# One decoder layer on one Trainium2 core: page-table reads spread among weight loads, state-space units with decays built in TensorE's weights, norms from a block of ones

## The chip, the core and the metric

The kernel runs on one core of one Trainium2 chip. A core has TensorE (PE, matrix products into PSUM), VectorE (DVE), ScalarE (ACT), GpSimd (POOL) and SyncE (SP), which here issues nearly all DMAs. Each engine runs its own instruction stream in order, and semaphores tie the streams together. The metric is the device time of one execution in microseconds (us), lower is better.

## The reference

One decoder layer for 512 prompt tokens and 8 samples of 8 new tokens (576 tokens, width 2048), all in fp32: one projection, sparse attention on one half of the heads, a Mamba-2 scan (SSD) on the other, an output projection, and a convolutional feed-forward layer, with RMS norms around both halves. Cut to what the change touches:

```python
def rmsnorm(x, g):
    y = x * lax.rsqrt(jnp.mean(x * x, -1, keepdims=True) + EPS)
    return y * g

def nsa_sample(...):                      # paged cache, 8 samples x 4 pages
    past = cache_kv_l[page_table].reshape(b, past_len, N_CACHE_SLOTS, KV_HEADS, HEAD_DIM)
    ...
    return o, win_all[:, -win_len:]       # win_sample: cache rows moved on by 8, and the new ones

# nsa_block, compressed branch: scores of every query with 31 blocks
s_c = jnp.einsum('btgrd,bngd->btgrn', q, kc) * SCALE + bias_c

def ssd_scan(x, a, bm, cm, h0):           # step, chunk of 128 tokens
    acum = jnp.cumsum(ac, axis=1)
    seg = acum[:, :, None] - acum[:, None]
    decay = jnp.where(causal, jnp.exp(jnp.where(causal, seg, 0.0)), 0.0)
    cb = jnp.einsum('bign,bjgn->bijg', cc, bc)
    y = jnp.einsum('bijg,bijgr,bjgrp->bigrp', cb, decay, xc)
    y = y + jnp.einsum('bign,bgrpn->bigrp', cc, h) * jnp.exp(acum)[..., None]
    h = (h * jnp.exp(acum[:, -1])[..., None, None]
         + jnp.einsum('bjgn,bjgrp->bgrpn', bc, xc * to_end[..., None]))

# block_tail
x = x + rmsnorm(mix, g_mix_post)
h = rmsnorm(x, g_ffn_pre)
```

## The kernel before

`build()` writes the whole layer as five streams by hand. Tokens are in five tiles (four of 128 rows, one of 64), or in two halves of 288 columns where features lie on partitions. Counters called `phase` join the engines between stages. The order within a stage is that of the code.

**Weight stream.** A weight unit is 128 rows of 512 columns. SP loads unit u into one of four buffers, once the low part of unit u-4 has been made (`unit`, L425 on). ACT makes the high part (L697), after PE has finished unit u-1; POOL makes the low part, and PE does three matmuls for one product (high x high, low x high, high x low). The stages with most time are these: `w_in`, then `w_out` (L2041), then the feed-forward layer (L1609 to L1611, L2119). The period is PE's.

**Page table.** After the last weight load of `w_in`, SP reads the 32 entries of the page table into registers (L456), one `value_load` each, then waits for phase 8 and loads the old states of the scan in 8 parts (L466). The registers are used later, for the loads of the cache rows.

**State loop.** For each of the 8 parts PE transposes the states (L1714), ACT copies them (L775), PE multiplies them with C for the samples (L1724), and multiplies `B_by_sequence` with `x_to_end` for the new states (L1740, 64 rows, 512 columns); DVE adds, SP stores. `B_by_sequence` is made by POOL (L1517), last in a chain of products that begins once the exps of ACT (L770) are there. DVE's copies before these exps (L1090, L1091) take the cumulated decays out of PSUM; the first goes into `a_cumulative`.

**SSM units.** 20 units w = 4 tile + group, each for four heads. `ssd_scores(w)`: PE makes C B^T (L1752, 128x128) and, per head, the cumulated decay over all partitions (L1754: weights are the column a of the head, broadcast, times a triangle of ones). `seg_unit(w)`: DVE subtracts `a_cumulative` and adds a mask of 0 and -1e30 (L1116, four operations). ACT takes the exp in place (L797). `mix_unit(w)`: DVE multiplies `seg` (SBUF) with the scores in PSUM (L1124). `ssd_out(w)`: PE makes the output (L1766), the part from the state (L1769) and the new state (L1771), in banks 4, 5 and 6, after `unit_done(w-1)`. `out_unit(w)`: DVE scales and adds (L1142 to L1147: five operations, two for tile 0 and for the samples). POOL gates the result with z (L1526), and ACT's `unit_squares(w)` (L791) sums the squares. DVE's order is seg(w), out(w-1), mix(w). PE's is scores(w+1), out(w). POOL makes three products of 128x1024 for the next tile (L1499, L1501, L1507) at each tile boundary. Two buffers of `seg` and of the banks alternate.

**Compressed scores.** For the prompt PE multiplies queries and 31 compressed keys: 16 heads x 4 tiles, 64 rows each, in two records per product (L1956). A pair of KV heads lies in the upper and lower 64 partitions (row group q = 0 or 64). The order is by head, so four products in a row use one row group. Four heads share a bank and one signal `C_mm`, after which DVE adds the bias and subtracts the maximum (L1303 to L1306). Ahead of that DVE fills `bias_c` (L1294, L1298) out of `bias_p`, which DMAs bring.

**Middle norms.** In the last block of `w_out` ACT squares each finished block of 128 features (L662) and DVE sums 15 of 16 (L1376). `square_sums` (L2051) then makes ten matmuls with a column of ones, which give the sums with tokens on partitions; `rs_small` (L1361 to L1365) divides by D, adds eps and inverts; ACT takes the root of 128x5 values (L925); `rs_rows2` (L2059) spreads them back over all partitions and into rows by five matmuls with the unit matrix. DVE's L1385 and L1386 use them. The second norm does the same with one sum (L1391, L2051, L1363 on, L961, L2059), and L1404 copies the rows to SBUF. An fp32 matmul shows as two records.

**Copies.** The 8 parts of `win_sample` that are taken over from the cache are DMAs of 1008 KB each from memory to memory, on SP's queue before the `w_out` loads (L541 to L543).

## Time and profile before

| | us |
| --- | --- |
| median of 3 runs | 3338.15 |
| the runs | 3348.89, 3338.15, 3336.52 |
| the profiled execution | 3346.54 |
| its span in the trace | 3344.4 |
| PE busy in it | 3109.9 (93%) |
| DVE, ACT, POOL busy | 1110.9, 1096.3, 1117.3 (33% each) |
| TensorE clock, mean | 0.942 of full |

The span runs from the first to the last instruction in the trace; 2.14 us lie outside. PE is busy nearly all the time in the weight stages. The middle stages lie from about 625 (end of the `w_in` stream) to 1366 (start of the `w_out` stream), and the middle norms at 1581 to 1655. A row of a timeline tells the start, the length, the engine, the line, the operation, output and inputs, how many were merged into the row, and in square brackets how long the engine idled before it and what released it. Times in this section's rows are us from the start of the span.

### The profile page before, as it was taken

How to read it: one execution, taken by the hardware profiler on the slowest of the kernel's cores; microseconds unless marked ns; L12 is line 12 of the kernel's file. 1: busy time of each engine (PE TensorE's matmuls, PEld its weight loads, DVE VectorE, ACT ScalarE, POOL GpSimd, SP SyncE). 2: the span in 40 equal slices, each digit the busy share in tenths (PEclk: the TensorE clock that was granted, in tenths of full speed). 3: DMA queues.
4: the chain of work that ended last, by engine and by line, in shares of the span. 5: the costliest groups of instructions: out<-in, count | busy, mean ns of one | idle time of the engine just before them, and what ended most of it. 6: DMA issues, size and time to landing. Idle time of an engine off the chain costs nothing.

```text
span 3344.4 us, 56486 instructions
## 1 busy us (share of the span) xinstructions
PE 3109.9 (93%) x21753; PEld 2893.2 (87%) x21753; DVE 1110.9 (33%) x1924; ACT 1096.3 (33%) x1980; POOL 1117.3 (33%) x911
## 2 busy tenths in 40 slices
PE   8999998977788789899799999999999999999997
PEld 7999776756685556799799999999999999999997
DVE  3145000016433365211532333323232333434344
ACT  4222222311223266322633333333333333333332
POOL 2444333223001022233444444444444434343342
PEclk9999999957698799999899999999999999999998
DMA  6333223131343700322322222222222222222233
GB/s 184 83 82 82 76 75 106 38 92 41 74 110 121 197 1 2 107 79 81 95 82 82 82 82 82 83 83 82 82 82 82 82 75 83 78 82 78 76 120 112
DMA packets 385732, 285.23 MB, mean 85 GB/s; under 512 B 95549, under 2 KB 321949, under 8 KB 384270
## 3 DMA queue, kind: packets, MB, share of 16 engines
q1 hardware_dynamic: 382152, 275.50, 29.1%
q10 hardware_dynamic: 3472, 8.26, 0.7%
q8 instruction: 71, 1.16, 0.2%
q14 instruction: 37, 0.30, 0.0%
HBM read 259.98 MB, written 31.97 MB: 87 GB/s over the span
## 4 chain that ended last, share of the span: by engine, by line
PE 67%; issue 16%; POOL 6%; DVE 4%; SPq 4%; ACT 3%; DMA 0%; POOLq 0%; DVEq 0%; ACTq 0%
PE ps L2119 17%; PE ps L1609 11%; PE ps L1611 11%; PE ps L1610 11%; POOL w_lo L1488 5%; PE ps L2041 5%; SPq L456 1%; SPq L521 1%; PE ps L2003 1%; PE ps L1969 1%; PE ps L1922 1%; ACT scores_p L883 1%; PE ps L1740 1%; ACT pT_prompt L894 1%; PE ps L1724 1%
## 5 line engine op out<-in xcount | busy, mean ns | idle before, releaser
L1560 POOL TENSOR_TENSOR w_lo<-w_raw,w_hi 128x512 fp32r<-128x512 f32 x572 | 737.3, 1289 | 1158.5 <-ACT w_hi L975 656.5
L1609 PE MATMUL ps<-hT_hi,w_hi 128*128 128x288 f32 x3520 | 1048.0, 298 | 3.4 <-DVE ffn_xr L1415 2.8
L1610 PE MATMUL ps<-hT_lo,w_hi 128*128 128x288 f32 x3520 | 1041.0, 296 | 0.0
L1611 PE MATMUL ps<-hT_hi,w_lo 128*128 128x288 f32 x3520 | 1037.3, 295 | 0.0
L1609 PEld LDWEIGHTS ps<-hT_hi,w_hi 128*128 128x128 f32 x3520 | 662.1, 188 | 5.2 <-POOL w_lo L1560 3.0
L1611 PEld LDWEIGHTS ps<-hT_hi,w_lo 128*128 128x128 f32 x3520 | 665.5, 189 | 0.0
L1610 PEld LDWEIGHTS ps<-hT_lo,w_hi 128*128 128x128 f32 x3520 | 663.5, 188 | 0.0
L975 ACT ACTIVATE w_hi<-w_raw 128x512 fp32r<-128x512 f32 x336 | 213.2, 635 | 716.8 <-PE ps L1611 716.8
L1488 POOL TENSOR_TENSOR w_lo<-w_raw,w_hi 128x512 fp32r<-128x512 f32 x176 | 233.1, 1325 | 397.8 <-ACT w_hi L697 397.8
L697 ACT ACTIVATE w_hi<-w_raw 128x512 fp32r<-128x512 f32 x250 | 157.9, 633 | 616.5 <-PE ps L1611 216.7
L680 DVE TENSOR_TENSOR act_lo<-ffn_act_T,act_hi 128x576 fp32r<-128x576 f32 x172 | 219.6, 1277 | 332.6 <-ACT act_hi L673 332.6
L2119 PE MATMUL ps<-act_hi,w_hi 128*128 128x288 f32 x1376 | 298.0, 299 | 15.4 <-DVE ffn_out_T L1440 10.7
L2119 PE MATMUL ps<-act_lo,w_hi 128*128 128x288 f32 x1376 | 297.7, 298 | 0.0
L2119 PE MATMUL ps<-act_hi,w_lo 128*128 128x288 f32 x1376 | 297.2, 298 | 0.0
L2119 PEld LDWEIGHTS ps<-act_hi,w_hi 128*128 128x128 f32 x1376 | 224.6, 191 | 16.2 <-issue 16.2
L671 ACT ACTIVATE w_hi<-w_raw 128x512 fp32r<-128x512 f32 x172 | 108.8, 632 | 360.2 <-PE ps L2119 353.2
L2119 PEld LDWEIGHTS ps<-act_lo,w_hi 128*128 128x128 f32 x1376 | 224.6, 191 | 0.0
L2119 PEld LDWEIGHTS ps<-act_hi,w_lo 128*128 128x128 f32 x1376 | 224.4, 191 | 0.0
L1669 PE MATMUL ps<-w_hi,hT_hi 128*128 128x512 f32 (+1 forms) x400 | 158.7, 397 | 16.0 <-POOL w_lo L1488 9.2
L1670 PE MATMUL ps<-w_hi,hT_lo 128*128 128x512 f32 (+1 forms) x400 | 157.4, 394 | 0.0
L1671 PE MATMUL ps<-w_lo,hT_hi 128*128 128x512 f32 (+1 forms) x400 | 156.1, 390 | 0.0
L1428 DVE TENSOR_TENSOR ffn_act_T<-ps,rs_rows_sb 128x576 f32 x43 | 32.6, 757 | 297.3 <-PE ps L1611 297.3
(368 smaller groups left out, 3888.4 us busy)
## 6 DMA issues: line engine op xcount, KB each, us to landing
w_raw<-in_ffn_w_gate SPq DMA_DIRECT2D x172, 256.0 KB, 2.8
w_raw<-in_ffn_w_up SPq DMA_DIRECT2D x172, 256.0 KB, 2.8
w_raw<-in_ffn_w_down SPq DMA_DIRECT2D x172, 256.0 KB, 2.6
w_raw<-in_w_in SPq DMA_DIRECT2D x144, 256.0 KB, 2.7
w_raw<-in_w_out SPq DMA_DIRECT2D x64, 256.0 KB, 2.6
w_raw<-in_w_in SPq DMA_DIRECT2D x64, 128.0 KB, 2.7
cmp_rows<-in_cache_kv SPq DMA_DIRECT2D x64, 128.0 KB, 3.2
kv_rows<-in_cache_kv SPq DMA_DIRECT2D x32, 256.0 KB
```

Of the source, the lines that this page charges most:

```text
L680: dve.tensor_tensor(a_lo[:, v % 2, :], src, a_hi[:, v % 2, :].bitcast(F32), ALU.subtract).then_inc(alo_done, 1)
L697: act.activation(w_hi[:, u % 2, :], w_raw[:, u % 4, :], ACT.Copy).then_inc(hi_done, 1)
L975: act.activation(w_hi[:, j % 2, :], w_raw[:, (U_FFN + j) % 4, :], ACT.Copy).then_inc(hi_done, 1)
L1488: pool.tensor_tensor(w_lo[:, j % 2, :], w_raw[:, j, :], w_hi[:, j % 2, :].bitcast(F32), ALU.subtract).then_inc(lo_done, 1)
L1560: pool.tensor_tensor(w_lo[:, u % 2, :], w_raw[:, u % 4, :], w_hi[:, u % 2, :].bitcast(F32), ALU.subtract).then_inc(lo_done, 1)
L1609: pe.matmul(o, W[0], X[0], start=(k == 0), stop=False)
L1610: pe.matmul(o, W[0], X[1], start=False, stop=False)
L1611: i = pe.matmul(o, W[1], X[0], start=False, stop=(k == KT - 1))
L1669: pe.matmul(o, X[0], W[0], start=(k == 0), stop=False)
L1670: pe.matmul(o, X[1], W[0], start=False, stop=False)
L2041: m = pe.matmul(ps[:, 2 * f + h, 0:HALF], W[wt], mix[:, k, HALF * h:HALF * h + HALF], start=(k == 0 and x == 0), stop=False, skip_group_ch ...
L2119: m = pe.matmul(ps[:, 2 * f + h, 0:HALF], W[wt], act_[:, v % 2, HALF * h:HALF * h + HALF], start=(k == 0 and x == 0), stop=False, skip_gro ...
```

## The change

1. The 32 reads of the page table stand behind one weight load each, for the units of c = 1 and 2 of the `w_in` stream, and no longer behind the last load.
2. In the SSM units the seg(w) of DVE is gone. ACT writes, per head, `decay_weights`: a mask of ones for k > i, times the head's a (`Copy` with a scale per partition, four operations of 128x128). PE uses it as weights against the triangle, so that PSUM holds the sum of a over the tokens between. ACT takes the exp from PSUM into `seg`. DVE's new `mask_unit` multiplies the scores with the triangle into `masked_scores`, and mix(w) multiplies two SBUF operands. DVE's order is mask(w), mix(w), out(w-1); ACT's is decay_weights(w+1), exp(w), squares(w-1). `ssd_out` alternates between banks 4 and 5, 6 and 7, and waits for `unit_done(w-2)`. The two copies to `a_cumulative` are gone.
3. The middle norms multiply the squares with a 128x128 block of ones, in two halves of 288 columns, which gives the sum on all partitions at once (ten matmuls for the first norm, over the sum of 12 squares and the last four; two for the second). ACT takes the root over 128x576 in PSUM with scale 1/D and bias eps; DVE takes the reciprocal over 128x576. The small matmuls, the small DVE operations and L1376 for the last three blocks go.
4. The eight copies of `win_sample` stand behind every eighth `w_out` load.
5. The compressed scores alternate between the row groups with each product. Banks 0 and 1 are signalled half way, banks 2 and 3 at the end.
6. The load of the sample gates counts on the same semaphore as the bias loads.

```diff
@@ SP
+            pages = [[None] * 4 for s in range(NB)]
             for c in range(5):
                 col = O_KV + 512 * c if c < 3 else O_Z + 512 * (c - 3)
                 for k in range(KT):
                     unit(U_KV + KT * c + k, dram(w_in, k * 128 * INW + col, [[INW, 128], [1, 512]]), 0)
+                    if 1 <= c < 3:
+                        s, p = 4 * (c - 1) + k // 4, k % 4
+                        pages[s][p] = sp.value_load(A["page_table"][s:s + 1, p:p + 1], min_val=0, max_val=39)
...
-            pages = [[sp.value_load(A["page_table"][s:s + 1, p:p + 1], min_val=0, max_val=39) for p in range(4)] for s in range(NB)]
...
                     unit(U_OUT + KT * c + k, dram(A["w_out"], k * 128 * D + 512 * c, [[D, 128], [1, 512]]), 0)
+                    if k % 8 == 4:
+                        s = 2 * c + k // 8
+                        sp.dma_start(O["win_sample"][0, s, 0:PAST - NT].rearrange("t s g d -> t (s g d)"),
+                                     A["cache_win_kv"][0, s, NT:PAST].rearrange("t s g d -> t (s g d)")).then_inc(y_stored, 16)
@@ ACT
+            def decay_weights(w):
+
+                t, g = w // 4, w % 4
+                n = TILES[t][1]
+                later = con[0:n, C_SL:C_SL + n] if t < 4 else con[0:n, C_SLS:C_SLS + n]
+                if w >= 2:
+                    act.wait_ge(s1_ready, w - 1)
+                for h in range(4):
+                    i = act.activation(decw[0:n, w % 2, h, 0:n], later, ACT.Copy, scale=a_[0:n, t, 4 * g + h:4 * g + h + 1])
+                i.then_inc(decw_ready, 1)
+
+            act.wait_ge(a_ready, 1)
+            decay_weights(0)
             for w in range(20):
                 n = TILES[w // 4][1]
-                act.wait_ge(seg_ready, w + 1)
-                act.activation(seg[0:n, w % 2, :, 0:n], seg[0:n, w % 2, :, 0:n], ACT.Exp).then_inc(dec_exp, 1)
+                if w < 19:
+                    decay_weights(w + 1)
+                act.wait_ge(s1_ready, w + 1)
+                if w >= 2:
+                    act.wait_ge(y_ready, w - 1)
+                act.activation(seg[0:n, w % 2, :, 0:n], ps[0:n, 2 + w % 2, :].rearrange("p (h i) -> p h i", h=4)[:, :, 0:n], ACT.Exp).then_inc(dec_exp, 1)
                 if w:
                     unit_squares(w - 1)
...
-            act.wait_ge(inv_ready, 2)
-            act.activation(rs, rs, ACT.Sqrt).then_inc(rs_ready, 1)
+            act.wait_ge(sum3_ready, 1)
+            act.activation(ps[:, 0:2, 0:HALF], ps[:, 0:2, 0:HALF], ACT.Sqrt, scale=1.0 / D, bias=eps_col).then_inc(rs_ready, 1)
@@ DVE
+            def mask_unit(w):
...
+                dve.tensor_tensor(scm[0:n, w % 2, 0:n], ps[0:n, w % 2, 0:n], earlier, ALU.mult).then_inc(scm_ready, 1)
...
                 dve.tensor_tensor(seg[0:n, w % 2, :, 0:n], seg[0:n, w % 2, :, 0:n],
-                                  ps[0:n, w % 2, 0:n].unsqueeze(1).broadcast_to([n, 4, n]), ALU.mult).then_inc(M_done, 1)
+                                  scm[0:n, w % 2, 0:n].unsqueeze(1).broadcast_to([n, 4, n]), ALU.mult).then_inc(M_done, 1)
...
             for w in range(21):
                 if w < 20:
-                    seg_unit(w)
+                    mask_unit(w)
+                    mix_unit(w)
                 if w >= 1:
                     out_unit(w - 1)
-                if w < 20:
-                    mix_unit(w)
...
-            dve.wait_ge(sum3_ready, 1)
-            rs_small(0)
-            dve.wait_ge(few_T, 6)
+            dve.wait_ge(rs_ready, 2)
             dve.wait_ge(y_evac, 16)
+            ch(dve.reciprocal(halves(flat(6)), ps[:, 0:2, 0:HALF]))
@@ PE
+                pe.wait_ge(decw_ready, w + 1)
...
-                    i = pe.matmul(ps[0:n, 2 + w % 2, 128 * h:128 * h + n], a_[0:n, t, 4 * g + h:4 * g + h + 1].broadcast_to([n, n]), tri, start=True, stop=True)
+                    i = pe.matmul(ps[0:n, 2 + w % 2, 128 * h:128 * h + n], decw[0:n, w % 2, h, 0:n], tri, start=True, stop=True)
...
+            for x in range(8):
                 for i in range(4):
...
+                    for par in range(2):
+                        h = 8 * (x // 4) + 4 * par + x % 4
+                        g, q = h // 4, 64 * par
...
+            def square_sums(bank, sq, first, last):
+
+                for h in range(2):
+                    i = pe.matmul(ps[:, bank + h, 0:HALF], every, sq[:, HALF * h:HALF * h + HALF], start=first, stop=last, skip_group_check=True)
+                if last:
+                    i.then_inc(sum3_ready, 1)
```

ACT's order in the SSM units before: `seg` is the exp of a unit, `squares_unused` the squares of the one before.

```order
L782 ACTIVATE ssd_small<-ps 128x8
L797 ACTIVATE seg<-seg 128x512 x2
L791 ACTIVATE squares_unused_88,ssd_small<-zs 128x256
L797 ACTIVATE seg<-seg 128x512
L791 ACTIVATE squares_unused_88,ssd_small<-zs 128x256
```

The same place now, where `decay_weights` are the four activations of a unit:

```order
L788 ACTIVATE ssd_small<-ps 128x8
L808 ACTIVATE decay_weights<-con,ssd_small 128x128 x8
L820 ACTIVATE seg<-ps 128x512
L808 ACTIVATE decay_weights<-con,ssd_small 128x128 x4
L820 ACTIVATE seg<-ps 128x512
L797 ACTIVATE squares_unused_89,ssd_small<-zs 128x256
L808 ACTIVATE decay_weights<-con,ssd_small 128x128 x4
L820 ACTIVATE seg<-ps 128x512
```

Between the squares of one unit and the exp of the next stand four activations that weren't there.

DVE in a unit of the tiles 1 to 3 before, from the subtraction of unit w over the five output operations of unit w-1 to its mix:

```order
L1116 SCALAR_TENSOR_TENSOR seg<-ps,a_cumulative,con 128x128 x4
L1142 TENSOR_TENSOR y_tmp<-ps,ssd_small 128x256
L1143 TENSOR_TENSOR h_state<-h_state,ssd_small 128x256
L1144 TENSOR_TENSOR xs_tok<-xs_tok,ps 128x256
L1146 TENSOR_TENSOR h_state<-h_state,ps 128x256
L1147 TENSOR_TENSOR xs_tok<-xs_tok,y_tmp 128x256
L1124 TENSOR_TENSOR seg<-seg,ps 128x512
```

And now:

```order
L1139 TENSOR_TENSOR masked_scores<-ps,con 128x128
L1146 TENSOR_TENSOR seg<-seg,masked_scores 128x512
L1164 TENSOR_TENSOR y_tmp<-ps,ssd_small 128x256
L1165 TENSOR_TENSOR h_state<-h_state,ssd_small 128x256
L1166 TENSOR_TENSOR xs_tok<-xs_tok,ps 128x256
L1168 TENSOR_TENSOR h_state<-h_state,ps 128x256
L1169 TENSOR_TENSOR xs_tok<-xs_tok,y_tmp 128x256
```

The mix has moved ahead of the output operations of the unit before, behind one product in place of four subtractions.

SP where the KV weights are loaded, now; before, all of these `TENSOR_LOAD` rows stood behind the last weight load:

```order
L435 DMA w_raw<-in_w_in 128x512 x17
L454 TENSOR_LOAD in_page_table_ptr
L454 TENSOR_LOAD in_page_table
L454 ISA x2
L435 DMA w_raw<-in_w_in 128x512
L454 TENSOR_LOAD in_page_table_ptr
```

One read stands between two loads of 128x512.

## Rows read from the trace of the kernel before

**Rows 1.** The page's chain of waits, by line: share of the span.

```profile
PE ps L2119 17%; PE ps L1609 11%; PE ps L1611 11%; PE ps L1610 11%; POOL w_lo L1488 5%; PE ps L2041 5%; SPq L456 1%; SPq L521 1%; PE ps L2003 1%; PE ps L1969 1%; PE ps L1922 1%; ACT scores_p L883 1%; PE ps L1740 1%; ACT pT_prompt L894 1%; PE ps L1724 1%
```

**Rows 2.** Timeline of SP, 620 to 690.

```profile
624.90 0.58 SPq L453 DMA_DIRECT2D w_raw<-in_w_in  x1
681.60 0.36 SPq L460 DMA_DIRECT2D norm_gain<-in_ssm_norm_g  x1
```

**Rows 3.** Timeline of PE, 664 to 701.

```profile
667.74 0.26 PE L1707 MATMUL ps<-ssd_small,con 64*64 64x16 f32 x2
688.12 1.94 PE L1714 MATMUL ps<-con,h 128*128 128x128 f32 x8 [20.12 <-DMA h<-in_state_ssm]
...
697.11 3.78 PE L1740 MATMUL ps<-B_by_sequence,x_to_end 64*128 64x512 f32 x4
```

**Rows 4.** Timeline of ACT in the w_in stream.

```profile
377.61 0.63 ACT L697 ACTIVATE w_hi<-w_raw 128x512 fp32r<-128x512 f32 x1 [2.80 <-PE ps L1671]
```

**Rows 5.** Timeline of POOL, 674 to 700.

```profile
679.53 1.89 POOL L1517 TENSOR_TENSOR B_by_sequence<-B_tok,con 64x1024 f32<-64x1024 f32 x1
```

**Rows 6.** Windows: from:to and length, busy us of the engines, clock, DMA share, GB/s.

```profile
670.00:671.00 1.00, 0.00 (x0) 0.00 (x0) 0.00 (x0) 0.00 (x0) 0.99 (x1) 0.60 0.00 0
688.00:768.00 80.00, 77.49 (x264) 53.33 (x264) 20.71 (x24) 10.52 (x24) 6.54 (x4) 0.50 0.32 88
```

**Rows 7.** Timeline of DVE, one SSM unit of tile 1.

```profile
802.48 0.68 DVE L1124 TENSOR_TENSOR seg<-seg,ps 128x512 f32<-128x512 f32 x1
803.08 1.12 DVE L1116 SCALAR_TENSOR_TENSOR seg<-ps,a_cumulative,con 128x128 f32<-128x128 f32 x4
805.28 0.42 DVE L1142 TENSOR_TENSOR y_tmp<-ps,ssd_small 128x256 f32<-128x256 f32 x1 [1.08 <-PE ps L1771]
```

**Rows 8.** Timelines of POOL and ACT, the same unit.

```profile
807.23 0.72 POOL L1526 TENSOR_TENSOR zs<-xs_tok,zs 128x256 f32<-128x256 f32 x1 [3.87 <-DVE xs_tok L1147]
...
807.99 0.42 ACT L791 ACTIVATE squares_unused<-zs 128x256 f32<-128x256 f32 x1 [3.13 <-POOL zs L1526]
...
808.82 0.63 ACT L797 ACTIVATE seg<-seg 128x512 f32<-128x512 f32 x1 [0.32 <-DVE seg L1116]
```

**Rows 9.** Timeline of ACT, 128x128 activations with a scale per partition.

```profile
1162.63 0.40 ACT L883 ACTIVATE scores_p<-scores_p,softmax_small 128x128 f32<-128x128 f32 x1 [0.57 <-DVE softmax_small L1324]
1162.94 0.19 ACT L883 ACTIVATION_READ_ACCUMULATOR scores_p<-scores_p,softmax_small 128x1 f32 x1
```

**Rows 10.** Timelines of DVE and POOL at a tile boundary.

```profile
788.08 1.87 DVE L1143 TENSOR_TENSOR h_state<-h_state,ssd_small 128x256 f32<-128x256 f32 x1
...
787.77 1.90 POOL L1501 TENSOR_TENSOR x_to_end<-x_dt,ssd_small 128x1024 f32<-128x1024 f32 x1
```

**Rows 11.** The mixes L1124 on DVE: count, lengths in ns, first and last start.

```profile
L1124 DVE TENSOR_TENSOR seg<-seg,ps x20: 405/680/686, 772.8 to 859.3; 128x512 f32<-128x512 f32 x16, 64x256 f32<-64x256 f32 x4
```

**Rows 12.** Timelines of PE and DVE, compressed scores of the prompt.

```profile
1135.84 23.25 PE L1956 MATMUL ps<-k_cmp_T,qT 64*128 64x31 f32 x128 [0.91 <-ACT K_T_prompt L875]
...
1145.94 0.68 DVE L1303 TENSOR_TENSOR probs_c_prompt<-ps,bias_c 128x496 f32<-128x496 f32 x1
...
1159.12 0.68 DVE L1303 TENSOR_TENSOR probs_c_prompt<-ps,bias_c 128x496 f32<-128x496 f32 x1 [3.70 <-PE ps L1956]
...
1161.47 1.22 PE L1969 MATMUL ps<-K_T_prompt,qT 64*128 64x128 f32 x8 [2.39 <-DVE probs_c_prompt L1306]
```

**Rows 13.** Timelines of ACT and DVE at the first middle norm.

```profile
1578.93 1.45 ACT L662 ACTIVATE mix_squares<-ps 128x576 f32<-128x576 f32 x2
...
1591.74 0.76 DVE L1385 TENSOR_TENSOR ps<-mix_out_T,ps 128x576 f32<-128x576 f32 x1 [3.08 <-PE ps L2059]
```

**Rows 14.** Reciprocals of DVE by form: busy, mean ns, idle before.

```profile
L1333 DVE RECIPROCAL softmax_small<-softmax_small 128x4 f32<-128x4 f32 x32 | 5.7, 178 | 1.1
...
L1313 DVE RECIPROCAL cmp_softmax_small<-cmp_softmax_small 128x16 f32<-128x16 f32 x4 | 1.0, 253 | 0.1
```

**Rows 15.** DMAs of 1130 to 1170: count, KB each, median us to landing.

```profile
w_raw<-in_w_out SPq DMA_DIRECT2D x4, 256.0 KB, 28.5
```

More of the change, by code:

```diff
@@ L72, in constants @@
     c[:64, C_TRIS:C_TRIS + 64] = same & (ks <= js)
-    c[:64, C_CBS:C_CBS + 64] = np.where(same & (ks <= js), 0.0, NEG)
+    c[:64, C_SLS:C_SLS + 64] = same & (ks > js)
     c[:64, C_SEQ:C_SEQ + 8] = ks // NT == np.arange(8)[None, :]
@@ L147, in build @@
         rs = small[:, 5:10]
+        eps_col = small[:, 38:39]
         gains = small[:, 112:176]
@@ L212, in build @@
         pool_ch = sem("pool_chain")
-        acs = at("a_cumulative", [128, NTT, NH], RX + 6656)
+        decw = at("decay_weights", [128, 2, 4, 128], RA + 31744)
+        scm = at("masked_scores", [128, 2, 128], RA + 35840)
         dec = sp_[:, 468:484].rearrange("p (b s) -> p b s", b=2)
@@ L371, in build @@
         ones = con[:, C_ONE:C_ONE + 1]
+        every = con[:, C_ONE:C_ONE + 128]
         x2r = at("x2", [128, NTT, D], RB)
@@ L959, in _ @@
                 x2_square(k)
-            act.wait_ge(inv_ready, 3)
-            act.activation(rs, rs, ACT.Sqrt).then_inc(rs_ready, 1)
+            act.wait_ge(sum3_ready, 2)
+            act.activation(ps[:, 6:8, 0:HALF], ps[:, 6:8, 0:HALF], ACT.Sqrt, scale=1.0 / D, bias=eps_col).then_inc(rs_ready, 1)
             act.sem_inc(phase, 1)
@@ L1024, in _ @@
             dve.wait_ge(small_zero, 1)
+            dve.memset(eps_col, EPS)
             dve.tensor_copy(gains, ps[:, 1, 0:64]).then_inc(small_zero, 1)
@@ L1952, in _ @@
             pe.wait_ge(kp_evac, 4)
[L1953 to L1954 removed]
+            for x in range(8):
                 for i in range(4):
[L1956 to L1959 removed]
+                    for par in range(2):
+                        h = 8 * (x // 4) + 4 * par + x % 4
+                        g, q = h // 4, 64 * par
+                        ins = pe.matmul(ps[:, h // 4, 124 * (h % 4) + NCMP * i:124 * (h % 4) + NCMP * i + NCMP],
+                                        qT[q:q + 64, 4 * (g // 2) + h % 4, 128 * i:128 * i + 128], kcT[q:q + 64, 8, g // 2, :], start=True, stop=True)
+                        if h % 4 == 3 and i == 3:
+                            ins.then_inc(C_mm, 1)
             def p_scores(S):
```

109 lines of the change are left out of this document (38 added, 71 removed).

## The prediction

> **What bounds the kernel now.** I read the chain of waits first: TensorE (PE) holds two thirds of it, nearly all in the weight stages, which the change leaves alone, and SP's page reads of L456 stand in it with 1% of the span although they are no work of the calculation [rows 1]. So the change can move time only where PE waits or runs sparse: the page reads, the state loop, the SSM units, the compressed scores and the two middle norms. The windows tell the clock there (during the state loop it is 0.50 of full, the lower level of 1.2 GHz) and the timelines the order of waits. The profiled execution took 3346.54 us, 8.4 above the median of the runs shown (3338.15); I work out a difference against the profiled one and apply it to the median.
>
> **Page reads.** SP issues the last weight load at 624.90 and the next DMA at 681.60 [rows 2]: with 0.6 for the issue, 56.1 us for 32 reads, 1.75 each. PE is done at 668.0, waits 20.12 for the states, and the state loop's first L1740 starts at 697.11 [rows 3]. Moved between the loads of weight units, a read costs SP 1.75 in a period of 0.63 + 2.80 = 3.43 [rows 4], of which the load's issue takes some 0.4 [rows 2]: hidden, since 3.43 is above 2.2. After it SP reaches the phase's wait at about 655, the states land by 661, and PE goes on at 668.0 instead of 688.12. From there to L1740 the transposes, ACT's copy and the y_off products took 9.0; 668.0 + 9.0 gives 677. But L1740 also reads B_by_sequence, which GpSimd (POOL) makes last of its chain, from 679.53 for 1.89, to 681.4 [rows 5]. That is next late; less 0.1 for the two removed copies of a_cumulative, 681.3. Gain 697.1 - 681.3 = **-15.8** (15 to 16). In between the clock fell at 670 to 671 [rows 6], while PE was idle. In the new order PE has matmuls of 8 columns there and another idle stretch of 4 us before 681; I take it that the state loop, 80 us with PE busy 77.5, stays at 0.50 as before [rows 6]. That is a choice: see rival A.
>
> **SSM units.** Before, DVE subtracts and masks (four operations, 1.12), ACT takes the exp, DVE mixes, PE makes the outputs, DVE's five output operations follow. Now the shift is done in PE, from weights that ACT writes (four 128x128 activations a unit), so 4 operations of DVE (1.12) go and one 128x128 mask product comes (about 0.2 by the same rows); ACT gains four operations. What matters is the order on ACT: exp(w), squares(w-1), decay_weights(w+2), exp(w+1). Squares(w-1) wait for POOL's z, that for DVE's out(w-1), which stands behind mix(w), and mix(w) for exp(w). That closes a ring, one turn per unit, none of which overlaps:
> exp start to mix start 0.66 (the exp of 128x512 at 808.82 is 0.63 long, and a semaphore) [rows 8]; mix to the next DVE operation, 802.48 to 803.08, 0.60 [rows 7]; first output operation 805.28 to POOL's z 807.23 to squares 807.99, 2.71 [rows 7, 8]; squares to ACT's next operation 0.41 (they are 0.42 long); four activations with a scale per partition. The nearest row for these is ACT's L883, also 128x128 with such a scale: from 1162.63 to its reading of the sum at 1162.94, a pitch of 0.31 [rows 9]; I take 0.30, 1.20 for four. Sum 5.6 us. For tile 0 out has two operations instead of five: 4.5.
> At each of three tile boundaries POOL's three long products (1.9 each) run beside DVE. L1143, with two operands in SBUF, took 1.87 at 788.08 while POOL's product of 787.77 ran, though it takes 0.41 elsewhere [rows 10]. Mix now has two operands in SBUF too (before, one in PSUM). I take 2.1 more at each boundary.
> The Trainium skill says so as a rule (SBUF — State Buffer, "Who interferes with whom"): a DVE instruction with two SBUF inputs and a GpSimd instruction that reads SBUF lock each other out for a whole instruction. The trace agrees with 1.87 against 0.41; by the rule the mixes of the boundaries are hit too, up to 1.6 each, which speaks against this change.
> Mix to mix, in order: 2.0 and 5.5 (nothing yet to be squared; then the start of the ring), 3 x 4.5, 9 x 5.6 with 3 x 2.1, and five about the last tile (64 rows, two output operations) that fall from 5.3 to 2.9, 21.9 together: 99.5. Before, first to last mix took 86.5 (772.8 to 859.3) [rows 11]. The first mix now starts 1.5 sooner after its scores (no subtraction ahead). So **+11.5**, slower. Bounds: activations of 0.22 instead of 0.30 give 4 x 0.08 x 19 = 6 less, all boundary stalls gone another 2.5: +3; 0.35 and a mix hit at every boundary +18. PE isn't in the ring: a unit has 1408 columns of fp32 matmuls, by L1740's price [rows 3] 5.2 us at half and 2.6 at full clock; with gaps I take 6.6 and 3.3, of which only the half clock would take over. That PE may now run a unit ahead gives nothing while the ring sets the pace.
>
> **Compressed scores.** The 64 products, 128 records, took 23.25 us from 1135.84, though each has but 31 columns: 0.18 a record, with 16 products running in one row group. At L1969, where the row groups alternate, eight records took 1.22, 0.153 each, though they have more columns [rows 12]. Alternated, 128 take at most some 19.5 us and end by 1155.4; the columns are fewer here, so more is to be had, and I take an end of about 1150. The Trainium skill has this as its rule that weight loads run under a matmul in flight only where the row groups differ (TensorE: Matmul & The Clock Gate, "The mechanism" of packing small matmuls); the trace agrees, 0.153 against 0.18. DVE takes 2.3 for each block of four heads, and its first starts at 1145.94, behind a memset that waits for the bias, not for PE; the last started at 1159.12, kept by PE, and 1161.4 was the end [rows 12]. Back to back 1145.94 + 4 x 2.3 = 1155.1: **-6.3**. But blocks 3 and 4 are now both told at the end: if PE ends only at 1155.4 they give 1155.4 + 4.6 = 1160.0, -1.4; if alternating brings nothing, 1159.1 + 4.6, 2.3 later than now.
>
> **Norms.** Before: 10 small matmuls, three DVE operations, a root, 10 matmuls, until L1385 at 1591.74. Now PE has 10 fp32 matmuls of 288 columns as soon as L2041 is done at 1581.2. The price of an fp32 matmul stands at L1740: two of 512 columns (four records) take 3.78 at the half clock [rows 3], so one of 288 takes 1.05 at half and 0.52 at full. PE comes out of the dense w_out stream, so I take the full clock: 5.2, end 1586.4; at half it would be 5.3 more. Root over 128x576 in PSUM 0.74, as the squares of that shape, two in 1.45 [rows 13]. DVE's reciprocal took 178 ns for 4 elements and 253 for 16 [rows 14]: 6.25 ns each, 3.75 us for 576, an extrapolation. End 1590.9, **-0.8** against 1591.74 [rows 13]. The second norm has two such matmuls instead of twenty, the same root and reciprocal: 1.1 + 0.8 + 3.75 = 5.6 after the last sum, about what the old chain of L2051, three DVE operations, root, L2059 and the copy takes there, 0. Together **-0.8**, bounds -7 (a reciprocal at one element a cycle as the other DVE operations of that shape, 0.76, in both) and +5.
>
> **Copies.** Before, the eight copies held the four w_out loads behind them for 28.5 us, where nobody needed them; so 3.5 a copy [rows 15]. Among the w_out loads each delays the next load by that, and loads run three units of over 3 us ahead: 0, cover 9 us. The merged semaphore and the eps memset are 0.
>
> Sum: -15.8 + 11.5 - 6.3 - 0.8 = **-11.4**; 3346.54 becomes 3335.1, the median 3326.8.
>
> **Rivals.** (A) The clock. With PE idle for only 4 us instead of 20 in two pieces it might not fall for the whole state loop. Then 77.5 us of PE work at half shrink, held up by SP's and DVE's parts of the loop, by perhaps a third: -25 more, -36. Against it: the clock was down for the whole 80 us in which PE was 97% busy [rows 6], so work alone didn't raise it here. 0.07. (B) The ring is not closed as I think, PE (3.3) paces the units: 20 x 3.3 = 66 instead of 102.3 (99.5 and the ends, 2.8), total -48. The instruction order speaks against it. 0.04. (C) The ring is cheap, +3: total -20. 0.17. (D) The reordered scores bring nothing and the activations are dear: scores 0, units +14: total -15.8 + 14 - 0.8 = -3. 0.10. (E) Slower than before: the page reads in the weight stream take longer than alone, as each waits for memory beside 256 KB loads. The point from which it decides: 3.43 - 0.4 = 3.0 us a read; SP's lead of three units gives some 9 us. At 4.5 us a read 31 x 1.45 - 9 = +36, total +25. The reads of before ran with no load beside them [rows 2], so nothing in the trace excludes it. 0.06.
>
> **How the numbers follow.** My case has 0.56, with its own range 3319 to 3335. What a measurement of this kernel can tell from no change is 0.5%, 16.7 us, so below 3321.5 is faster. A, B, C hold 0.28, of my case 0.04 falls there: faster 0.32. E 0.06 and 0.01 of mine: slower 0.07. The rest 0.61. The range reaches over C and D, 3312 to 3341, and leaves A, B and E out.
>
> **What would show it.** Page reads: first L1740 near 681, released by POOL, no idle of PE for a DMA. Units: period of mix 5.6 (wrong if under 4.6), exp released by ACT's own row, DVE idle before out small, PE idle over 2 us a unit. Scores: last block's maximum at about 1155, relative to the stage's start. Norms: two reciprocals of 3.7 us. Clock in the state loop 0.50. Wrong would be a period of 3.43 in the weight stage that grows, or a full clock after 681.

## The result and the profile after

| | before | changed |
| --- | --- | --- |
| median, 20 runs each | 3342.80 | 3335.72 |
| lowest, highest | 3327.66, 3349.24 | 3325.86, 3343.27 |
| profiled execution's span | 3344.4 | 3332.5 |
| TensorE clock in it, mean | 0.942 | 0.944 |

The ratio is 0.998, with a 95% interval from 0.997 to 0.9989: some 7 us faster (4 to 10), 0.2%. The forecast was -0.34% (-11.4 us), and it called everything within 0.5% the same as no change. The time of 3335.72 lies in the range of 3312 to 3341. But the kernel did get faster, by more than its interval and by less than the sum of the forecast. The spans of the two profiled executions differ by 11.9 us. That this is close to the -11.4 of the forecast is chance: runs of one kernel scatter by some 20 us, and it is the stages that have to be compared, not the spans.

| stage, between starts on PE | before | changed | forecast | measured |
| --- | --- | --- | --- | --- |
| last sums over a (L1707, 667.8 before) to first product of new states (L1740) | 29.3 | 14.7 | -15.8 | -14.6 |
| state loop, first product to last | 68.9 | 68.8 | 0 | 0 |
| first scores of the units (L1752) to the first transposition after them (L1781) | 93.5 | 107.3 | +11.5 | +13.8 |
| first compressed score (L1956) to first window score (L1969) | 25.6 | 20.6 | -6.3 | -5.0 |
| first w_out matmul to last | 214.1 | 216.1 | 0 | +2.0 |
| last w_out matmul to first transposition of x (L2076) | 12.3 | 11.3 | -0.8 | -1.0 |
| from there to the first matmul of w_down, second norm in it | 1144.4 | 1144.4 | 0 | 0 |

The four terms that the edits can explain give -14.6 + 13.8 - 5.0 - 1.0 = -6.8, near the 7.1 by which the medians differ. That they meet so well is in part luck, since each side is one execution and a stage with the same code differs by 1 to 8 us between executions, as the experiments show. All seven rows give -4.8; the other 7.1 of the 11.9 lie in stages whose code is the same. For one, the attention of the samples, from its first transposition to the last, took 128.6 us before and 124.9 after. The windows over it (from:to and length; busy us of PE, PEld, DVE, ACT, POOL; clock, DMA share, GB/s), first of before, then of the changed kernel:

```profile
1003.00:1132.00 129.00, 106.90 (x649) 68.37 (x649) 41.18 (x165) 39.84 (x96) 9.56 (x24) 0.85 0.47 126
```

```profile
1001.00:1127.00 126.00, 103.53 (x653) 66.92 (x652) 41.39 (x166) 39.73 (x96) 9.56 (x24) 0.88 0.50 135
```

The work is the same; the clock granted to it is not. The kernels of the experiments with that stage unchanged show 123.7 to 131.8 us.

**State loop.** The rows that answer to [rows 3], timeline of PE in the changed kernel:

```profile
665.53 0.27 PE L1719 MATMUL ps<-ssd_small,con 64*64 64x16 f32 x2
665.99 1.09 PE L1726 MATMUL ps<-con,h 128*128 128x128 f32 x8 [0.19 <-ACT B_tok L774]
...
674.21 0.42 PE L1746 MATMUL ps<-con,y_off_T 128*64 128x128 f32 x1
680.27 3.78 PE L1752 MATMUL ps<-B_by_sequence,x_to_end 64*128 64x512 f32 x4 [5.64 <-POOL B_by_sequence L1529]
```

and of POOL, which answers to [rows 5]:

```profile
673.62 1.90 POOL L1513 TENSOR_TENSOR x_to_end<-x_dt,ssd_small 128x1024 f32<-128x1024 f32 x1
675.48 2.88 POOL L1519 TENSOR_TENSOR xs_tok<-xs_tok,small 128x1024 f32<-128x1024 f32 x1
678.32 1.89 POOL L1529 TENSOR_TENSOR B_by_sequence<-B_tok,con 64x1024 f32<-64x1024 f32 x1
```

The wait for the state's DMA is gone, and POOL is next late, as forecast. POOL's product of 675.48, the fifth of the chain, took 2.88 and not 1.90. DVE's first product of the state loop, on two operands in SBUF, now falls beside it:

```profile
674.94 1.66 DVE L1126 TENSOR_TENSOR h<-h,ssd_small 128x1024 f32<-128x1024 f32 x1
```

It started first and ends at 676.60, and POOL's comes out 1.0 longer: most of the 1.2 us that are missing from the 15.8. In `best_copies_in_stream` (below) the order of POOL's products is another, and there it is the product of 676.64 that meets DVE's first one and takes 2.76, while the one that is stretched here is back at its usual length:

```profile
676.64 2.76 POOL L1513 TENSOR_TENSOR x_to_end<-x_dt,ssd_small 128x1024 f32<-128x1024 f32 x1
679.37 1.90 POOL L1519 TENSOR_TENSOR xs_tok<-xs_tok,small 128x1024 f32<-128x1024 f32 x1
```

So the length goes with the meeting and not with the instruction. The clock of the loop, 680 to 752, as in [rows 6], behind two windows ahead of it:

```profile
667.00:668.00 1.00, 0.08 (x1) 0.00 (x0) 0.00 (x0) 0.99 (x3) 0.18 (x1) 1.00 0.00 0
669.00:670.00 1.00, 1.00 (x6) 1.00 (x6) 0.00 (x0) 0.00 (x0) 0.92 (x2) 0.50 0.00 0
680.00:752.00 72.00, 70.03 (x229) 46.66 (x230) 19.67 (x22) 10.50 (x28) 7.59 (x5) 0.50 0.32 88
```

It is 0.50 again; rival A is out. The clock had fallen before the idle stretch of 5.64 us, which the prediction had at 4 and gave as a reason: it was 1.00 from 667 to 668 and 0.50 from 669 on, with PE idle for only 1.53 us between (L1736 of 668.61 waits for ACT's copy). In `best_copies_in_stream` these 1.53 us are the only idle time there, and the loop stays at 0.50 all the same.

**SSM units.** A turn of tile 1, on ACT and on DVE (L1146 is the mix):

```profile
788.16 0.42 ACT L797 ACTIVATE squares_unused<-zs 128x256 f32<-128x256 f32 x1 [3.35 <-POOL zs L1538]
788.49 0.19 ACT L797 ACTIVATION_READ_ACCUMULATOR squares_unused<-zs 128x1 f32 x1
788.58 1.26 ACT L808 ACTIVATE decay_weights<-con,ssd_small 128x128 f32<-128x128 f32 x4
789.75 0.57 ACT L820 ACTIVATE seg<-ps 128x512 f32<-128x512 f32 x1
```

```profile
784.85 0.69 DVE L1146 TENSOR_TENSOR seg<-seg,masked_scores 128x512 f32<-128x512 f32 x1 [2.82 <-ACT seg L820]
785.46 0.42 DVE L1164 TENSOR_TENSOR y_tmp<-ps,ssd_small 128x256 f32<-128x256 f32 x1
785.79 0.41 DVE L1165 TENSOR_TENSOR h_state<-h_state,ssd_small 128x256 f32<-128x256 f32 x1
786.13 0.41 DVE L1166 TENSOR_TENSOR xs_tok<-xs_tok,ps 128x256 f32<-128x256 f32 x1
786.57 0.42 DVE L1168 TENSOR_TENSOR h_state<-h_state,ps 128x256 f32<-128x256 f32 x1
786.91 0.42 DVE L1169 TENSOR_TENSOR xs_tok<-xs_tok,y_tmp 128x256 f32<-128x256 f32 x1
787.24 0.28 DVE L1139 TENSOR_TENSOR masked_scores<-ps,con 128x128 f32<-128x128 f32 x1
790.35 0.69 DVE L1146 TENSOR_TENSOR seg<-seg,masked_scores 128x512 f32<-128x512 f32 x1 [2.83 <-ACT seg L820]
```

Mix to mix is 5.50 us. ACT waits 3.35 for z and then runs without a gap through squares, decays and exp; DVE waits 2.83 for that exp. Each waits while the other, or POOL, works: that is the ring. Before, the same pitch was 4.59 (802.48 to 807.07).

At a tile boundary, the same engine:

```profile
776.51 2.16 DVE L1146 TENSOR_TENSOR seg<-seg,masked_scores 128x512 f32<-128x512 f32 x1 [2.83 <-ACT seg L820]
778.59 0.41 DVE L1164 TENSOR_TENSOR y_tmp<-ps,ssd_small 128x256 f32<-128x256 f32 x1
778.92 1.78 DVE L1165 TENSOR_TENSOR h_state<-h_state,ssd_small 128x256 f32<-128x256 f32 x1
```

Mix and L1165 are both stretched, by 1.47 and 1.37 us, 2.84 together, and the mix-to-mix time is 8.34, which is 5.50 + 2.84. The same happens at all three boundaries. The second turn, from the mix of 756.89 to that of 763.37, took 6.48. PE in it, first in this kernel and then in `copies_back`, whose units have the same code:

```profile
756.62 1.97 PE L1779 MATMUL ps<-x_dt,seg 128*128 128x64 f32 x8 [0.40 <-DVE seg L1146]
758.39 1.17 PE L1784 MATMUL ps<-x_to_end,B_tok 128*128 128x256 f32 x2
```

```profile
757.57 1.19 PE L1778 MATMUL ps<-x_dt,seg 128*128 128x64 f32 x8 [0.40 <-DVE seg L1145]
758.61 0.65 PE L1783 MATMUL ps<-x_to_end,B_tok 128*128 128x256 f32 x2
```

From 758 to 760 the granted clock is 0.50 here and 1.00 there. There the turn took 5.23.

**Compressed scores**, PE and then DVE, which answer to [rows 12]:

```profile
1130.58 11.87 PE L1971 MATMUL ps<-k_cmp_T,qT 64*128 64x31 f32 x128 [0.91 <-ACT K_T_prompt L898]
1151.22 1.23 PE L1984 MATMUL ps<-K_T_prompt,qT 64*128 64x128 f32 x8 [8.77 <-DVE probs_c_prompt L1327]
```

```profile
1139.04 1.71 DVE L1315 MEMSET bias_c<- 128x1984 f32 x1 [11.43 <-DMA bias_p<-bias_scratch]
...
1142.26 0.68 DVE L1324 TENSOR_TENSOR probs_c_prompt<-ps,bias_c 128x496 f32<-128x496 f32 x1
...
1150.49 0.67 DVE L1327 TENSOR_TENSOR probs_c_prompt<-probs_c_prompt,cmp_softmax_small 128x496 f32<-128x496 f32 x1
```

PE needs 11.87 us for the 128 records instead of 23.25, and stands idle for 8.77 then. DVE runs its four blocks back to back from 1142.26, 11.7 after the stage's start; that start is set by the bias load. In the seven other kernels with this order and this fill it lies 9.0 to 12.7 us after the stage's start, so a part of the -5.0 is where the load happened to land.

**First norm**, PE, ACT, DVE:

```profile
1571.28 4.04 PE L2065 MATMUL ps<-mix_squares,con 128*128 128x288 f32 x16
...
1575.36 0.71 ACT L948 ACTIVATE ps<-ps,small 128x576 f32<-128x576 f32 x1 [2.17 <-PE ps L2065]
...
1576.11 3.77 DVE L1394 RECIPROCAL ps<-ps 128x576 f32<-128x576 f32 x1 [4.10 <-ACT ps L948]
```

The matmuls took 5.0 in all, the root 0.71 and the reciprocal 3.77, against 5.2, 0.74 and 3.75 of the forecast.

### The profile page after: what moved, and what is told of

It is laid out like the page before. It is cut to its first block, busy times and chain, and to the rows that moved or that the text cites. A ratio compares the mean times of both kernels' runs of the same rounds, so it can differ in the third digit from the quotient of the medians.

```text
span 3332.5 us, 56502 instructions
## 1 busy us (share of the span) xinstructions
PE 3095.4 (93%) x21727; PEld 2878.2 (86%) x21727; DVE 1101.2 (33%) x1855; ACT 1117.1 (34%) x2060; POOL 1119.3 (34%) x911
## 3 DMA queue, kind: packets, MB, share of 16 engines
q1 hardware_dynamic: 382152, 275.50, 29.3%
q8 instruction: 71, 1.16, 0.2%
## 4 chain that ended last, share of the span: by engine, by line
PE 68%; issue 14%; POOL 6%; ACT 5%; DVE 4%; SPq 2%; DMA 0%; POOLq 0%; DVEq 0%; ACTq 0%
PE ps L2124 17%; PE ps L1621 11%; PE ps L1623 11%; PE ps L1622 11%; PE ps L2056 5%; POOL w_lo L1500 5%; SPq L526 1%; PE ps L1984 1%; PE ps L2018 1%; PE ps L1681 1%; PE ps L1935 1%; PE ps L1682 1%; PE ps L1683 1%; ACT scores_p L906 1%; PE ps L1752 1%
```

## Experiments

The times of the experiments are ratios to the kernel before, timed on the same chip; a difference to the changed kernel is the difference of the ratios (its own is 0.998), times 3340 us. The intervals of the ratios are 0.12 to 0.25% (4 to 8 us) to either side, and a difference of two of them is known to some 5 to 9 us, so a verdict rests on the stage in the profile and is borne out by the ratio. The units' stage took 107.3 us in the changed kernel, but 106.0 to 106.1 in the three kernels that leave the units alone (`pages_back`, `cscores_back`, `copies_back`), because the second turn takes 5.1 to 5.3 there.

### Each part undone

**Page reads back behind the last load** (`pages_back`).

```diff
-                    if 1 <= c < 3:
-                        s, p = 4 * (c - 1) + k // 4, k % 4
-                        pages[s][p] = sp.value_load(...)
...
+            pages = [[sp.value_load(...) for p in range(4)] for s in range(NB)]
             sp.wait_ge(phase, 8)
```

> The changed kernel with the 32 page-table reads back behind the last weight load. Theory: from PE's last sums over a to its first product for the new states it takes 29.3 us again instead of 14.7: total +14.6 us. Rival: the reads between the weight loads cost the w_in stream something that the medians feel; then the total moves by less than 10, and the w_in stage (342 to 635) shortens by the rest.

Ratio 1.0027 (1.0014 to 1.0041), 16 us above the changed kernel. From the last sums to the first product it takes 29.1 us. The w_in stage, first matmul to last, takes 292.8 with the reads behind it and 292.4 with the reads in it: they cost that stream nothing. Rival E is out.

**SSM units as before, all else kept** (`units_old`).

```diff
-                    mask_unit(w)
-                    mix_unit(w)
+                    seg_unit(w)
                 if w >= 1:
                     out_unit(w - 1)
+                if w < 20:
+                    mix_unit(w)
```

> The changed kernel with the SSM units as before (subtraction and mask on DVE, exp in place, single output banks), all other parts kept. Theory: the stage from first scores to the end of the units goes back from 107.3 to 93.5 us, total -13.8 us against the changed kernel, so some -20 against the kernel before. Rival: the units cost less than the one profiled execution says (clock of that execution), and the total moves by under 5.

Ratio 0.9941 (0.9926 to 0.9956), 13 us below the changed kernel. The stage of the units took 91.2 us, where the same units took 93.5 in the kernel before. Over all these kernels (91.2 and 93.5 against 106.0 to 107.3) the new units lose 12.5 to 16 us. The other parts together bring some 20 us, nearly three times what the whole change brings.

**Compressed scores in the old order** (`cscores_back`).

```diff
-            for x in range(8):
+            for h in range(NH):
+                g, q = h // 4, 64 * (h // 4 % 2)
                 for i in range(4):
-                    for par in range(2):
```

> The changed kernel with the compressed scores in the old order, by head, the signals one bank at a time. Theory: PE takes 22.9 us for them instead of 11.5 and DVE's last blocks wait for PE again; from the first compressed score to the first window score it takes 25.7 us again instead of 20.6, total +5. Rival: the stage hangs on the bias loads, which end when they end, and the order gives 2 us or less.

In this order 16 products in a row (four heads, four tiles) use one row group, not four as the description of the kernel before has it. Ratio 1.0004 (0.9986 to 1.0022), 8 us above the changed kernel, with an interval as wide. PE takes 25.0 us for the scores, at a granted clock of 0.50, and the stage takes 27.5. In the eight kernels that have the new order and no edit of DVE's fill the same stage takes 17.9 to 21.7 us, 20.0 in the mean, since it depends on when the bias lands; so against the 25.6 of before and the 27.5 here the order is worth some 5.6 to 7.5. A row of DVE there shows the wait for PE that the new order removes:

```profile
1165.90 0.68 DVE L1324 TENSOR_TENSOR probs_c_prompt<-ps,bias_c 128x496 f32<-128x496 f32 x1 [3.70 <-PE ps L1969]
```

**Cache copies back ahead of the w_out loads** (`copies_back`).

```diff
-                    if k % 8 == 4:
-                        s = 2 * c + k // 8
-                        sp.dma_start(O["win_sample"]..., A["cache_win_kv"]...)
...
             sp.wait_ge(phase, 20)
+            for s in range(NB):
+                sp.dma_start(O["win_sample"]..., A["cache_win_kv"]...)
```

> The changed kernel with the eight cache copies back ahead of the first w_out loads. Theory A, read from one pair of profiles: the copies between the w_out loads cost the w_out stage 2 us (216.1 against 214.1), so -2. Theory B, from four other profiles with the copies in the stream (214.8 to 216.4): the stage scatters by itself and the copies cost 1 or nothing; then it lies between 214 and 216 here too. In front of the stage, the eight copies run beside the bias loads: where these are what the compressed softmax waits for, that stage grows from 20 to 21 or 22 us.

Ratio 0.9977 (0.996 to 0.9995), 1 us from the changed kernel. The w_out stage took 215.8. With the copies in the stream the other kernels show 214.8 to 218.0, with the copies ahead 214.1 to 216.3 (means 216.3 of ten kernels and 215.4 of three): they scatter over each other, and the means differ by 0.9, less than the kernels of one kind among themselves; so the +2.0 of the table above can't be laid to the copies. The first part of theory B holds; that the copies ahead slow the bias loads isn't decided, with 21.6 us for that stage in this kernel and 21.7 in `pages_back` too.

### The ring

**Squares one turn later** (`squares_late`).

```diff
-                if w:
-                    unit_squares(w - 1)
+                if w >= 2:
+                    unit_squares(w - 2)
+            unit_squares(18)
             unit_squares(19)
```

> The changed kernel with one edit: ACT takes the squares of a unit one turn later, squares(w-2) behind exp(w) and no longer squares(w-1). Theory: in the changed kernel the units are paced by a ring exp(w) - mix(w) - output operations of w-1 - z on POOL - squares(w-1) - decay_weights(w+2) - exp(w+1), 5.50 us a turn in the profile. With the squares of an older unit the ring is open, and the pace falls to PE's own work and DVE's: 3.3 to 3.8 us a unit in tiles 1 to 3, the stage from first scores to the end of the units from 107.3 to about 80 us, total -27 us. Rival: PE or the ping-pong of two buffers sets the pace already, and the ring only reads like one: the pitch stays above 5.2 and the total moves by less than 3 us.

Ratio 0.9875 (0.9861 to 0.9889), 35 us below the changed kernel. The stage of the units takes 75.3 us instead of 107.3. DVE, tile 1:

```profile
772.91 1.04 DVE L1147 TENSOR_TENSOR seg<-seg,masked_scores 128x512 f32<-128x512 f32 x1
...
775.66 0.28 DVE L1140 TENSOR_TENSOR masked_scores<-ps,con 128x128 f32<-128x128 f32 x1
776.04 1.05 DVE L1147 TENSOR_TENSOR seg<-seg,masked_scores 128x512 f32<-128x512 f32 x1
```

The pitch is 3.13 in tile 1, with DVE busy throughout. The rival of PE's pace falls: nothing but the order of ACT's stream was changed. With the ring open other limits show. The mixes of this pitch take 1.04 or 1.05 instead of 0.69, and from 787.75 to the last tile it is 3.4 to 5.4 from mix to mix, with waits of DVE for PE of up to 2.20 us; from 803 to 825 PE's granted clock is 0.59.

**Decays ahead of the squares** (`decays_first`).

```diff
-                if w < 19:
-                    decay_weights(w + 1)
...
                 act.activation(seg..., ACT.Exp).then_inc(dec_exp, 1)
+                if w < 18:
+                    decay_weights(w + 2)
                 if w:
                     unit_squares(w - 1)
```

> The changed kernel with one edit of order on ACT: decay_weights(w+2) behind exp(w) and ahead of squares(w-1), instead of behind them. Theory: in the changed kernel the four activations (1.17 us) stand in the ring; ahead of the squares they run while ACT would wait for z. The pitch of tiles 1 to 3 falls from 5.50 to 4.3 to 4.4, that of tile 0 from 4.38 to 3.4, the stage of the units from 107 to 87 to 90, total -17 to -20 against the changed kernel. Rival: with that the wait for scores(w+1), which decay_weights(w+2) needs, holds ACT up, or PE's pace does, and the pitch stays above 5.

Ratio 0.9941 (0.9929 to 0.9953), 13 us below; the stage takes 88.8 us. ACT:

```profile
783.46 0.42 ACT L797 ACTIVATE squares_unused<-zs 128x256 f32<-128x256 f32 x1 [2.19 <-POOL zs L1539]
783.78 0.19 ACT L797 ACTIVATION_READ_ACCUMULATOR squares_unused<-zs 128x1 f32 x1
783.88 0.58 ACT L819 ACTIVATE seg<-ps 128x512 f32<-128x512 f32 x1
784.35 1.27 ACT L808 ACTIVATE decay_weights<-con,ssd_small 128x128 f32<-128x128 f32 x4
787.80 0.42 ACT L797 ACTIVATE squares_unused<-zs 128x256 f32<-128x256 f32 x1 [2.18 <-POOL zs L1539]
```

The turn is 4.34, less than 5.50 by just the four activations, 1.16; what is left of the ring still holds it: ACT still waits 2.18 for z. Tile 0 turned in 3.22.

**Fewer decays** (`half_decay`).

```diff
-                for h in range(4):
+                for h in range(4 if w < 2 else 2):
                     i = act.activation(decw[...], later, ACT.Copy, scale=...)
```

> The changed kernel, but ACT writes decay_weights for all four heads only in units 0 and 1, and for heads 0 and 1 in the others (the decays of heads 2 and 3 are those of units 0 and 1, so that part of the computation is left out). Theory: the activations stand in the ring, each 0.29 us: the pitch of tiles 1 to 3 falls from 5.50 to 4.9, the units' stage by some 17 x 0.58 = 10 us, total -10. Rival (PE or DVE paces the units): no change of the pitch.

Ratio 0.9957 (0.9944 to 0.997), 8 us below; the pitch is 4.92 (mixes at 793.86 and 798.78), 0.58 less and so just two activations, and the stage takes 95.3, 12 less. The ring shortens by what is taken out of it, as in `decays_first`. That the stage lost 12 and not the 10 that were expected has two reasons beyond the pitch: the second turn took 4.72 instead of 6.48, and a boundary 7.29 instead of 8.34, with a mix of 0.77 that met only the end of a product of POOL.

**Masked scores in PSUM** (`mask_in_psum`).

```diff
-                dve.tensor_tensor(scm[...], ps[0:n, w % 2, 0:n], earlier, ALU.mult)
+                dve.tensor_tensor(ps[0:n, w % 2, 0:n], ps[0:n, w % 2, 0:n], earlier, ALU.mult)
...
-                                  scm[...].unsqueeze(1)...
+                                  ps[0:n, w % 2, 0:n].unsqueeze(1)...
```

> The changed kernel, but the masked scores are written back into their PSUM bank, and mix reads them there, so that it has one operand in SBUF and not two. Theory: the mix that met POOL's long products at the three tile boundaries took 2.16 instead of 0.69 (and the first one 1.81); in this form it takes 0.69 there, the mix-to-mix time across a boundary falls from 8.34 to 6.9 (L1165 of 1.78 stays), total -4 to -6. Rival: the boundary is set by the wait for POOL's products themselves, and the stall moves to the next operation: no change of the 8.34.

Ratio 0.9967 (0.9955 to 0.9979), 4 us below; the stage takes 101.6, 5.7 less. DVE at the same boundary as above:

```profile
776.03 0.69 DVE L1145 TENSOR_TENSOR seg<-seg,ps 128x512 f32<-128x512 f32 x1 [2.43 <-ACT seg L819]
776.63 0.42 DVE L1163 TENSOR_TENSOR y_tmp<-ps,ssd_small 128x256 f32<-128x256 f32 x1
776.96 0.96 DVE L1164 TENSOR_TENSOR h_state<-h_state,ssd_small 128x256 f32<-128x256 f32 x1
...
778.63 1.34 DVE L1168 TENSOR_TENSOR xs_tok<-xs_tok,y_tmp 128x256 f32<-128x256 f32 x1
```

The mix takes 0.69 where it took 2.16, and the time across the boundary (776.03 to 782.99) 6.96 instead of 8.34. The mix's stall did belong to the form of its operands. This is the rule of the Trainium skill that the prediction weighed (SBUF — State Buffer, "Who interferes with whom"), and the pair of 2.16 and 0.69 agrees with it.

But the expected 6.9 came out in another way than expected, and that is luck. The next product with two operands in SBUF (L1164, L1165 in the changed kernel) did not keep its 1.78 but took 0.96, and the one after it (L1168) took 1.34 instead of 0.42, as it now meets POOL's third long product. The stretches add up to 0.55 + 0.92 = 1.47 instead of 2.84. So a part of the stall did move to a later operation, as the rival had it, though not all of it.

### A version that beats both

Three edits of order on the changed kernel (`best_copies_in_stream`): the late squares; `B_by_sequence` for group 0 ahead of POOL's products of tile 0; the fill of `bias_c` ahead of DVE's wait for the bias.

```diff
             x_scaled(0, 4, 64, 0)
-            x_scaled(1, 0, 128, 1)
-            skip_scaled(0)
             for g in range(NG):
+                if g == 1:
+                    x_scaled(1, 0, 128, 1)
+                    skip_scaled(0)
...
-            dve.wait_ge(ld_TT, 512)
             dve.memset(cmb[:], MASKED).then_inc(v_ready, 1)
+            dve.wait_ge(ld_TT, 512)
```

> The changed kernel with three edits of order: squares(w-2) on ACT; POOL makes B_by_sequence before the products of tile 0; DVE fills bias_c before it waits for the bias loads. Theory: -37 for the squares as measured; the first product for the new states waited 5.64 us for B_by_sequence, which is now ready at 673.5 instead of 680.2: the 14.3 us from the first state transposes to that product fall to 9.0, -5.3; the memset of 1.71 stood behind a wait for a DMA: -1.7. Total -44 against the changed kernel, about 3291. Rival: the two products of tile 0 that now come later hold the SSM units up (scores of unit 0 wait for nothing of them, but the first outputs do), and give back up to 5.

Ratio 0.985 (0.9824 to 0.9875). The first product for the new states comes 8.5 us after the first transposition (14.3 in the changed kernel), with no wait for POOL, and the units' stage takes 73.9. What the earlier fill of `bias_c` brings isn't shown: the stage of the compressed scores takes 18.7, which lies among the 17.9 to 21.7 of the kernels without that edit. With the copies ahead of the loads:

> As the kernel with three edits of order, and the cache copies back ahead of the w_out loads. Tells the copies apart once more, at the other end of the total: theory A 2 us less than that kernel, theory B the same within 1.

Ratio 0.9857 (0.9832 to 0.9881), the same within the intervals; a difference of 2 us, as in theory A, would not be seen in them. With the masked scores in PSUM as well:

> The kernel with three edits of order, and the masked scores in PSUM as well. Theory: there the pitch of 3.1 has DVE busy nearly throughout, and mixes of 1.05 instead of 0.69 where they meet POOL's z; so -1.5 a boundary and -0.3 for each of some eight units: the units' stage from 73.9 to 66 to 69 us, total some 3288. Rival: PE at the clock it is granted there sets the pace, and the stage stays above 71.

Ratio 0.9854 (0.984 to 0.9868), median 3288.12, the lowest of all. The units' stage takes 67.6, within what was expected. By the total it can't be told from the two without that edit, by the stage it can.

## Where the prediction failed, and what of it held

The order of the waits was forecast rightly in every stage; what failed are sizes in the sum, and the price put on what a measurement can tell.

- **Page reads: right path, a term short.** The wait for the DMA went and POOL's chain was next late, at 680.2. The gain is 14.6 and not 15.8, since POOL's fifth product was stretched from 1.90 to 2.88 by DVE's work that is now beside it, and since the two copies that were taken out (0.1) gave nothing: POOL starts 2.3 us after the last sums as before. The prediction took POOL's chain as a constant, although the row at a tile boundary [rows 10] had shown what happens when the two meet.
- **Clock in the state loop: right value.** 0.50 as before; rival A (0.07) would have been wrong. But the clock had fallen by 669, before the idle stretch that the prediction named, so that reason was not needed.
- **SSM units: right mechanism, size too small.** The ring was forecast at 5.6 and is 5.50; tile 0 at 4.5 and is 4.38; the last five turns at 5.3 down to 2.9, 21.9 together, and they are 5.29 to 2.84, 21.8. Three terms were mis-sized. The boundaries were priced at 2.1 more and cost 2.84, because the sum took in the stretched L1165 but only part of the stretched mix, which the prediction had named and set in the bounds: 3 x 0.74 = 2.2. The second turn took 6.48 instead of 5.5, as PE was at the lower clock then; this belongs to the execution, since three other kernels with the same units took 5.1 to 5.3. Together 3.2, less 1.1 for the slightly shorter turns: from first to last mix 101.6 and not 99.5. And the first mix came 1.2 sooner after its scores, not 1.5. That the ring sets the pace isn't only argued: three edits on ACT alone moved the pitch of tile 1 to 3.13, 4.34 and 4.92.
- **Compressed scores: right path, two numbers off.** PE's end was put at about 1150, a choice that no row gave, and came 11.9 us after the start, which would be 1147.7 on the old scale; the pitch of L1969 was a poor measure for a product of 31 columns. It cost nothing, since DVE and the bias load are the limit, as forecast. The -6.3 came out as -5.0 since the bias landed later against the stage's start (DVE's first block 11.7 after it instead of 10.1). The prediction took that landing as fixed to the stage, and it isn't: it lies anywhere from 8.4 to 12.7 over the kernels.
- **Norms: right.** -0.8 forecast, -1.0 measured; the extrapolated reciprocal, 3.75, is 3.77. The second norm is even.
- **Copies: right**, 0 within what the runs can tell.
- **The sum.** 2.3 of the units, 1.2 of the page reads and 1.3 of the scores all went one way, 0.2 of the norms the other, and -11.4 became -6.8. The step that failed is the sum's treatment of engines that meet at new times. Two of its terms are DVE and POOL stretched by each other: the boundary, priced at 2.1 and measured at 2.84, and POOL's product, taken as 1.90 and measured at 2.88. The third is the landing of the bias, taken as fixed.
- **What a measurement can tell: wrong.** The prediction took 0.5% (16.7 us) as the least change to be told from none, which no row gave, and so put 0.61 on "no change", with its own sum of -11.4 under that line. With 20 runs of each the ratio is known to 0.1% (3 us) to either side, and 0.2% was told apart. A gain of 11.4 or of 6.8 us should both have been called faster.
- **The level.** The forecast median of 3326.8 started from a median of three runs, 3338.15; that of twenty is 3342.80. Of the 8.9 us between forecast and measured time 4.6 come from there and 4.3 from the change. That 3335.72 lies in the range owes much to the range's width of 29 us.

What stays open: why stages with the same code differ by up to 8 us between executions, along with the granted clock (sample attention 123.7 to 131.8), and whether the copies ahead of the w_out loads delay the bias.

## What to carry to other kernels

Follow the order of one engine's stream through every instruction of a turn, and ask of each what it waits for: a step that nobody needs soon (the squares) closed a ring through three engines (ACT, DVE and POOL), and any work that is put behind it (the decays) is paid in full. Moved by one turn it gave back 35 us here, five times what the whole change had brought. And where the profile shows a pair of engines that stretch each other, price every new pair that the change brings together, in the sum and not only in the bounds. Before calling a forecast "no change", work out from the number and the scatter of the runs what change they can tell.

## What the runs showed of the hardware

- DVE's reciprocal has a price of its own: 3.77 us for 128x576, where a product of that shape takes 0.76. A root on ACT of the same shape takes 0.71.
- An activation of 128x128 with a scale per partition has a pitch of 0.29 us (four in 1.26, the last one's end included).
- Products of 31 columns with alternating row groups took 0.093 us a record (128 in 11.87, granted clock 0.59), against 0.18 with 16 products in a row in one row group (23.25 in all, clock 0.54; 25.0 at 0.50 in `cscores_back`) and 0.153 for the wider ones of L1969.
- 32 reads of registers from memory took 56.1 us at the end of the stream, and between weight loads they cost nothing that could be seen (292.4 against 292.8 us).
- PE was 97% busy for 72 us in the state loop and its granted clock stayed at 0.50, the level of 1.2 GHz, although PE's idle time ahead of it fell from 20.12 us in one piece to 1.53 and 5.64, and to 1.53 alone in `best_copies_in_stream`.
- When a product of POOL and one of DVE that reads two operands in SBUF overlap, each of the two can come out longer: POOL's 128x1024 product took 2.88 instead of 1.90 and DVE's 1.66 instead of 1.21. At the boundaries DVE's mix took 2.16 instead of 0.69, and 0.69 with one operand in PSUM.
